# Attention scores from high and low parts of q and k in three fp32r products, and one chunk of a projection moved ahead of them

## The chip, the cores and the metric

The kernel runs on one core of a Trainium2 chip. The metric is the time of one execution on the device in microseconds (us), the median of several runs. The engines are TensorE (PE in the rows; PEld are its weight loads), VectorE (DVE), ScalarE (ACT), GpSimd (POOL) and SyncE (SP, which issues DMAs). Each works through its own list of instructions in order and waits on semaphores for the others.

## The reference

One layer of a hybrid decoder, for 528 prompt positions (16 learned meta tokens and 512 tokens) and 8 decoded tokens, 536 columns in all, d_model 1024, in float32:

```
x = x + 1/2 * SwiGLU_1(RMSNorm(x))
z = RMSNorm(x) @ w_in          -> u (pool group, 512) | q (8 heads of 64) | k | v (2 heads of 64)
q, k: RMSNorm over the head, rotation of the first quarter of the head
pool group: causal trailing means over 2/4/8/16 positions minus the token, a linear map per group, a scale
attention: sliding window of 128 in blocks of 128 queries x 256 keys, sinks:
  s = einsum('bnqhgd,bnkhd->bnhgqk', qb, k_band) * SCALE        (q, k in float32)
  p = exp(s - m) / (sum(exp(s - m)) + exp(sink - m));   o = p @ v
x = x + concat(pool, attention) @ w_out
x = x + 1/2 * SwiGLU_2(RMSNorm(x))
```

## The kernel before

Activations lie transposed: 128 channels on the partitions, positions along the free dimension. Wherever a product is large, both operands are kept as a high part (the value rounded to fp32r) and a low part (value minus high part), and three fp32r matmuls, hi x hi, lo x hi and hi x lo, are added up in PSUM (`product`, L612). ACT makes the high parts by a copy to fp32r, DVE the low parts by a subtraction (`split_hi`, `split_lo`).

The change is in the mixing stage between the two half FFNs, some 100 of the 877 us. Ten projections of w_in run in the order k, v, q0 to q3, u0 to u3 (`project(m, ks)`, m from 0 to 9), each of eight chunks of 128 rows of w_in; `ks` says which chunks, so that a projection can be cut and other work of TensorE put between. q0 to q3 each hold two heads, one on partitions 0 to 63 and one on 64 to 127, and so does k.

For x from 1 to 4 (q0 to q3; x = 0 is k) the way from a projection to the scores is: DVE evacuates it into `gate` (`take_z(x)`), ACT writes the gained values `zg` and the squares `zsq` (`spread_z(x)`), SP sends four DMAs that put the rotation's partner rows into `partner` (`send_partner(x)`), GpSimd multiplies `zg` by the cosines into `hid`, DVE multiplies `partner` by the sines into `sq` (`rotate(x)`, L1862), and GpSimd adds the two (L2123) into `qT`. For x = 0 the sum stays in `hid`, and DVE multiplies it by the inverse norm into `kT` (L1868). `zg`, `zsq` and `partner` have two buffers each, `hid` and `sq` one. The norm of q goes into the scores as a factor (`qscale`).

There are eight steps of attention, i = 0 to 7: block t = i % 4 of 128 queries, and two heads of each group, q0 and q1 for i < 4, q2 and q3 after. Of each step TensorE does `scores(i)` (four products of 64 rows, 128 x 256, L960, in plain fp32), `turn_probs(i)` (eight transposes, L969) and `attend(i)` (L978). DVE does `maxima(i)` (L1913 to L1919) and `normalise(i)` (L1925 to L1930, writes `prob`), ACT `exps(i)` (L1393), `out_probT(i)` (L1401, PSUM to `probT`) and `out_hi(i)`, DVE `out_lo(i)`. `attend(i)` waits for `probT`, `turn_probs(i)` for `prob`.

Each engine's order is written out by hand. TensorE around the first steps:

```
project(4, [5, 6, 7]); project(5, half[0]); scores(0); scores(1)
project(5, half[1]); project(6, half[0])
turn_probs(0); scores(2); project(6, [4]); attend(0); project(6, [5]); ...
turn_probs(1); scores(3); attend(1); ...
```

Steps 3, 4 and 6 run `turn_probs`, `scores` of the next step, `attend` without a break; steps 5 and 7 have `pool_map` (L933) between `turn_probs` and `scores`. (Steps are named here by their scores.) DVE runs `rotate(2)`, the reciprocal of the first norms, `take_z(3)`, `split_next(4)`, `maxima(0)`, `rotate(3)`, `maxima(1)`, `normalise(0)`, `take_z(4)`, `normalise(1)`. ACT runs `spread_z(2)`, `q_root(0)`, `split_next(4)`, `spread_z(3)`, `exps(0)`, `exps(1)`, `spread_z(4)`, `out_probT(0)`. After q3's add GpSimd copies the decoded tokens' queries into `dq` (L2129) and goes on to the pool group's window sums (L2106).

Of the kernel before, what the change touches and what calls it, by code (L numbers as in the profile page):

```python
# [39 lines left out]
P = 128  # L40
# [108 lines left out]
def build(nc, a):  # L149
# [52 lines left out]
    assert prob_end <= t4_end  # L202
    sq, _ = place("sq", [P, NT])
    sqsum, _ = place("sqsum", [P, NT])
    fixed, _ = place("fixed", [P, N_FIXED])
# [31 lines left out]
    qT, o = place("qT", [P, GQ, NOUT], offset=xlo_end)  # L237
# [26 lines left out]
    dscore, o = place("dscore", [HD, P], offset=o)  # L264
    assert o <= raw_at
# [71 lines left out]
    dq_ready = sem("dq_ready")  # L337
    dscores_filled = sem("dscores_filled")
# [261 lines left out]
    def _(pe):  # L600
# [320 lines left out]
        project(5, half[0])  # L921
# [15 lines left out]
        def scores(i):  # L937

            t = i % QT
            if i == 0:  # L940
                pe.wait_ge(rot_ready, 3)
                pe.wait_ge(root_ready, 4)
            elif i == 2:
                pe.wait_ge(evacuated, E_USE["q3"] + 1)
            elif i > 2:
                pe.wait_ge(olo_ready, i - 2)
            if i == 3:
                pe.wait_ge(root_ready, 5)
            elif i == 4:
                pe.wait_ge(rot_ready, 5)  # L950
# [6 lines left out]
            for k in (0, 2, 1, 3):  # L957
                g, j = head_of(i, k)
                rows = slice(g * HD, (g + 1) * HD)
                last = nc.tensor.matmul(dst[k], qT[rows, j, t * P:(t + 1) * P], kT[rows, t * P:(t + 2) * P],  # L960
                                        start=True, stop=True)
                if j % 2:
                    last.then_inc(scored, 1)
# [20 lines left out]
        def decode_scores(part):  # L984

            if part == 0:
                pe.wait_ge(newk_placed, 1)
                pe.wait_ge(dq_ready, KVH)
# [52 lines left out]
        project(5, half[1])  # L1041
# [69 lines left out]
    def _(act):  # L1111
# [275 lines left out]

        def exps(i):
# [31 lines left out]
        spread_z(2)  # L1420

# [5 lines left out]

        q_root(0).then_inc(root_ready, 1)
        act.wait_ge(warmed, 2)
        nc.scalar.activation(warm[:, :], eps[:, :], ACT.Exp).then_inc(warmed, 1)  # L1430
        split_next(4)
        spread_z(3)
        exps(0)
        exps(1)
        spread_z(4)
# [9 lines left out]
        out_probT(1)  # L1445
        split_next(6)
# [66 lines left out]
    def _(dve):  # L1513
# [357 lines left out]

        def pool_mean(g):
# [91 lines left out]
        nc.vector.tensor_copy(ckT[:, :, WIN - 1], kT[:, PAD + TP:PAD + NT]).then_inc(newk_placed, 1)  # L1964
        rotate(2)
        dve.wait_ge(root_ready, 4)
        half_q = QT * KVH * 2
        nc.vector.reciprocal(qnrm[:, 1, 0:half_q], qnrm[:, 0, 0:half_q]).then_inc(inv_ready, 1)
        take_z(3)
        split_next(4)  # L1970
# [19 lines left out]
        maxima(3)  # L1990
        dve.wait_ge(dscores_filled, 1)
# [97 lines left out]
    def _(pool):  # L2089
# [23 lines left out]
        for x in range(5):  # L2113
            cols = slice(0 if x == 0 else META, NT)
            pool.wait_ge(zg_ready, x + 1)
            if x == 1:
                pool.wait_ge(qk_ready, 1)
            nc.gpsimd.tensor_tensor(hid[:, cols], zg[:, x % 2, cols], cosT[:, cols], ALU.mult
# [3 lines left out]
            dst = hid[:, :] if x == 0 else qT[:, x - 1, :]  # L2122
# [113 lines left out]
```

## Time and profile before

| | us |
|---|---|
| median of 3 runs (879.41 to 879.66) | 879.43 |
| the profiled execution's own time | 879.43 |
| its span, from the first to the last instruction | 877.5 |
| TensorE busy | 872.0 (99%) |
| DVE busy | 659.4 (75%) |
| ACT busy | 394.0 (45%) |
| GpSimd busy | 32.4 (4%) |

The span is the profile's; the time of an execution has 1.9 us more around it. Times in rows are counted from the span's start. The ends of matmuls are modelled, and neighbours overlap in the rows, so what an operation of TensorE costs is read from start to start. A row of the timeline gives in brackets how long the engine was idle before it, and who released it.

### The profile page before, as it was taken

Reading aid. Unit: us, or ns where it says so; the run is one execution under the profiler, and the core shown is the slowest. Engines: PE = TensorE matmul, PEld = TensorE weight load, DVE = VectorE, ACT = ScalarE, POOL = GpSimd, SP = SyncE. Lnnn points to the kernel's source line nnn. Section 1 sums busy time; section 2 is a strip of 40 time slices with the busy share of each in tenths; the row PEclk is TensorE's granted clock in tenths of the full one; section 3 lists DMA queues with packets and bytes.
Section 4 is the critical chain, followed back from the end, with each engine's and each line's share of the span. In section 5 each row is a group of like instructions: output and inputs, shape, how many; then the busy total and the mean of one; then the engine's idle time right before and its main releaser. Section 6 shows DMA issues by size and latency. Waiting matters only on the chain.

```text
span 877.5 us, 17072 instructions
## 1 busy us (share of the span) xinstructions
PE 872.0 (99%) x7088; PEld 857.4 (98%) x7088; DVE 659.4 (75%) x979; ACT 394.0 (45%) x639; POOL 32.4 (4%) x37
## 2 busy tenths in 40 slices
PE   9999999999999999999999999999999999999998
PEld 8999999999999999999888999999999999999998
DVE  7979547997569986754887697996479975799754
ACT  8635313554224553443754465554125542255420
POOL 0000000000000000012423000000000000000000
PEclk9999999999999999999999999999999999999999
DMA  7333313332424322522321405324233324333241
GB/s 261 107 121 117 136 60 121 121 121 85 145 68 162 121 77 84 190 76 59 106 73 62 155 27 169 120 82 172 73 121 120 121 85 145 115 122 124 85 122 61
DMA packets 43180, 98.57 MB, mean 112 GB/s; under 512 B 4288, under 2 KB 5056, under 8 KB 43104
## 3 DMA queue, kind: packets, MB, share of 16 engines
q1 hardware_dynamic: 41376, 95.01, 32.7%
q10 hardware_dynamic: 1728, 2.48, 0.8%
q8 instruction: 56, 0.92, 0.4%
q14 instruction: 20, 0.16, 0.1%
HBM read 93.53 MB, written 3.60 MB: 111 GB/s over the span
## 4 chain that ended last, share of the span: by engine, by line
PE 97%; DVE 1%; DMA 1%; issue 0%; ACT 0%; SPq 0%; DVEq 0%
PE ps L612 45%; PE ps L740 15%; PE ps L742 15%; PE ps L741 15%; PE ps L642 1%; PE ps L978 1%; PE ps L960 1%; PE ps L969 1%; PE ps L799 1%; DMA raw<-gu 1%; PE ps L933 0%; PE ps L883 0%; PE ps L657 0%; DVE wlo L1533 0%; DVE hlo L1660 0%; DVE hid L1653 0%
## 5 line engine op out<-in xcount | busy, mean ns | idle before, releaser
L740 PE MATMUL ps<-xhi,whi 128*128 128x260 f32 (+1 forms) x1092 | 310.2, 284 | 0.1
L742 PE MATMUL ps<-xhi,wlo 128*128 128x260 f32 (+1 forms) x1092 | 310.0, 284 | 0.0
L741 PE MATMUL ps<-xlo,whi 128*128 128x260 f32 (+1 forms) x1092 | 309.5, 283 | 0.0
L740 PEld LDWEIGHTS ps<-xhi,whi 128*128 128x128 f32 x1092 | 205.3, 188 | 0.8 <-issue 0.6
L742 PEld LDWEIGHTS ps<-xhi,wlo 128*128 128x128 f32 x1092 | 205.4, 188 | 0.0
L741 PEld LDWEIGHTS ps<-xlo,whi 128*128 128x128 f32 x1092 | 205.4, 188 | 0.0
L1604 DVE TENSOR_TENSOR wlo<-full,whi 128x1024 fp32r<-128x1024 f32 (+1 forms) x117 | 160.4, 1395 | 0.0
L1129 ACT CAST whi<-raw 128x1024 fp32r<-128x1024 f32 (+1 forms) x75 | 75.2, 1003 | 154.9 <-PE ps L612 148.0
L612 PE MATMUL ps<-hhi,whi 128*128 128x268 f32 (+1 forms) x690 | 140.4, 285 | 0.3
L612 PE MATMUL ps<-hlo,whi 128*128 128x268 f32 (+1 forms) x690 | 140.1, 284 | 0.0
L612 PE MATMUL ps<-hhi,wlo 128*128 128x268 f32 (+1 forms) x690 | 139.7, 284 | 0.0
L612 PEld LDWEIGHTS ps<-hhi,whi 128*128 128x128 f32 x690 | 106.8, 188 | 1.1 <-DVE hlo L1660 1.1
L612 PEld LDWEIGHTS ps<-hhi,wlo 128*128 128x128 f32 x690 | 107.0, 188 | 0.0
L612 PEld LDWEIGHTS ps<-hlo,whi 128*128 128x128 f32 x690 | 106.8, 188 | 0.0
L1533 DVE TENSOR_TENSOR wlo<-raw,whi 128x1024 fp32r<-128x1024 f32 (+1 forms) x75 | 90.3, 1205 | 16.8 <-ACT whi L1129 16.5
L1700 DVE SCALAR_TENSOR_TENSOR gate<-ps,rstd 128x536 f32<-128x536 f32 (+1 forms) x47 | 33.3, 708 | 81.7 <-PE ps L612 81.2
L1189 ACT CAST whi<-full 128x1024 fp32r<-128x1024 f32 x39 | 41.0, 1052 | 106.3 <-issue 89.5
L612 PE MATMUL ps<-xhi,whi 128*128 128x268 f32 (+1 forms) x288 | 60.9, 293 | 0.0
L612 PE MATMUL ps<-xhi,wlo 128*128 128x268 f32 (+1 forms) x288 | 58.7, 285 | 0.0
L612 PE MATMUL ps<-xlo,whi 128*128 128x268 f32 (+1 forms) x288 | 58.5, 285 | 0.0
L1203 ACT CAST whi<-full 128x1536 fp32r<-128x1536 f32 x39 | 57.8, 1483 | 0.0
L1589 DVE TENSOR_TENSOR full<-full 128x1024 f32<-128x1024 f32 x39 | 47.4, 1217 | 0.0
(194 smaller groups left out, 1071.1 us busy)
## 6 DMA issues: line engine op xcount, KB each, us to landing
full<-gu SPq DMA_DIRECT2D x78, 512.0 KB, 4.3
raw<-d SPq DMA_DIRECT2D x32, 448.0 KB, 3.3
full<-gu SPq DMA_DIRECT2D x39, 256.0 KB, 2.7
raw<-d SPq DMA_DIRECT2D x16, 512.0 KB, 3.4
raw<-w_in SPq DMA_DIRECT2D x10, 512.0 KB, 3.7
raw<-gu SPq DMA_DIRECT2D x9, 512.0 KB, 3.7
raw<-w_out SPq DMA_DIRECT2D x8, 512.0 KB, 3.9
xT<-x SPq DMA_DIRECT2D x8, 268.0 KB, 5.5
```

What stands on the lines that cost most here:

```text
L612: last = nc.tensor.matmul(dst[:, h, 0:n], w[:, kk, :], x(k, lo, h), start=(k == begin and i == 0), stop=(k == end and i == 2))
L642: done = nc.tensor.matmul(dst[:, h, 0:n], w[:, c % 2, t, :], x(k, lo, h), start=(first and t == 0 and i == 0), stop=(last and t == KD - 1 ...
L740: nc.tensor.matmul(dst, whi_t, xhi_t, start=(first and pr == 0), stop=False, skip_group_check=True)
L741: nc.tensor.matmul(dst, whi_t, xlo_t, start=False, stop=False, skip_group_check=True)
L742: last = nc.tensor.matmul(dst, wlo_t, xhi_t, start=False, stop=(pr == KC - 1), skip_group_check=True)
L1129: nc.scalar.copy(whi_of(c)[:, 0:t, :], raw[:, c % RAW, 0:t, :]).then_inc(whi_ready, 1)
L1189: nc.scalar.copy(whi7[:, i % 2, 0:2, :], full[:, i % 3, 0:2, :]).then_inc(hi_ready[0], 1)
L1203: nc.scalar.copy(whi7[:, i % 2, 4:7, :], full[:, i % 3, 4:7, :]).then_inc(hi_ready[2], 1)
L1533: nc.vector.tensor_tensor(wlo_of(c)[:, 0:t, :], raw[:, c % RAW, 0:t, :], whi_of(c)[:, 0:t, :].bitcast(F32), ALU.subtract).then_inc(wlo_rea ...
L1589: nc.vector.tensor_tensor(full[:, r, 1:5:3, :], full[:, r, 1:5:3, :], full[:, r, 0:7:6, :], ALU.add).then_inc(added, 1)
L1604: nc.vector.tensor_tensor(wlo7[:, i % 3, b, :], full[:, i % 3, b, :], whi7[:, i % 2, b, :].bitcast(F32), ALU.subtract).then_inc(lo_ready[g ...
L1700: nc.vector.scalar_tensor_tensor(out=halves(gate[:, cols], n), in0=pair[d % 2][:, :, 0:n], scalar=-0.5, in1=halves(rstd[:, cols], n), op0= ...
```

## The change

The scores are computed from high and low parts: `khi`, `klo` for all of k, `qhi[:, j]` and `qlo[j]` for the 520 columns of each q. Each of the four fp32 products of a step becomes three fp32r matmuls of the same shape (hi x hi, lo x hi, hi x lo), interleaved by pairs of heads so that neighbours lie on different halves of the rows. GpSimd's add now leaves every q in `hid`; ACT copies it into `qhi` (`q_hi(x)`), and DVE (x = 1, 2, 4) or GpSimd (x = 3) subtracts to get `qlo` (`q_lo(x)`). Since `hid` is one buffer, GpSimd's multiply for the next q waits for the low part of the one before. ACT copies `kT` into `khi`, DVE subtracts to get `klo`. `dq` is filled after each q by two small copies, instead of two larger ones at the end. On TensorE, five chunks of `project(5)` now lie ahead of the first scores instead of four, and three behind them. The new tiles lie over buffers that are free in this stage.

```diff
@@ -918,7 +930,7 @@
         project(4, [2, 3, 4])
         q_sums(1)
         project(4, [5, 6, 7])
-        project(5, half[0])
+        project(5, [0, 1, 2, 3, 4])
 
         def use(name):
 
@@ -938,7 +950,9 @@
 
             t = i % QT
             if i == 0:
-                pe.wait_ge(rot_ready, 3)
+                pe.wait_ge(klo_ready, 1)
+                pe.wait_ge(qlo_ready[0], 1)
+                pe.wait_ge(qlo_ready[1], 1)
                 pe.wait_ge(root_ready, 4)
             elif i == 2:
                 pe.wait_ge(evacuated, E_USE["q3"] + 1)
@@ -947,20 +961,25 @@
             if i == 3:
                 pe.wait_ge(root_ready, 5)
             elif i == 4:
-                pe.wait_ge(rot_ready, 5)
+                pe.wait_ge(qlo_ready[2], 1)
+                pe.wait_ge(qlo_ready[3], 1)
                 pe.wait_ge(dscores_kept, 2)
             elif i == 6:
                 pe.wait_ge(dprobs_kept, 1)
             elif i == 7:
                 pe.wait_ge(douts_kept, 1)
             dst = [banks_of[i % 3][:, j // 2, (j % 2) * 2 * P:(j % 2 + 1) * 2 * P] for j in range(GQ)]
-            for k in (0, 2, 1, 3):
-                g, j = head_of(i, k)
-                rows = slice(g * HD, (g + 1) * HD)
-                last = nc.tensor.matmul(dst[k], qT[rows, j, t * P:(t + 1) * P], kT[rows, t * P:(t + 2) * P],
-                                        start=True, stop=True)
-                if j % 2:
-                    last.then_inc(scored, 1)
+            queries, keys = slice(t * P, (t + 1) * P), slice(t * P, (t + 2) * P)
+            for pair_of_heads in ((0, 2), (1, 3)):
+                for part in range(3):
+                    for k in pair_of_heads:
+                        g, j = head_of(i, k)
+                        rows = slice(g * HD, (g + 1) * HD)
+                        q = qlo[j][rows, queries] if part == 1 else qhi[rows, j, queries]
+                        last = nc.tensor.matmul(dst[k], q, (klo if part == 2 else khi)[rows, keys],
+                                                start=(part == 0), stop=(part == 2))
+                        if part == 2 and j % 2:
+                            last.then_inc(scored, 1)
 
         def turn_probs(i):
             pe.wait_ge(prob_ready, i + 1)
@@ -985,7 +1004,7 @@
 
             if part == 0:
                 pe.wait_ge(newk_placed, 1)
-                pe.wait_ge(dq_ready, KVH)
+                pe.wait_ge(dq_ready, KVH * GQ)
                 pe.wait_ge(probT_ready, 2)
             for b in range(part * NDEC // 2, (part + 1) * NDEC // 2):
                 last = nc.tensor.matmul(turn[:, 1, b * HEADS:(b + 1) * HEADS], ckT[:, b, :], dq[:, b, :, :],
@@ -1038,7 +1057,7 @@
 
         scores(0)
         scores(1)
-        project(5, half[1])
+        project(5, [5, 6, 7])
         project(6, half[0])
 
         turn_probs(0)
@@ -1385,6 +1404,11 @@
                 sq_x = nc.scalar.activation(dzsq[:, :, x - 1], gate[:, TP:NT], ACT.Square)
             sq_x.then_inc(zg_ready, 1)
 
+        def q_hi(x):
+
+            act.wait_ge(rot_ready, x + 1)
+            nc.scalar.copy(qhi[:, x - 1, :], hid[:, META:NT]).then_inc(qhi_ready, 1)
+
         def exps(i):
             act.wait_ge(nmax_ready, i + 1)
             s = i % 2
@@ -1418,6 +1442,9 @@
         spread_z(1)
         split_next(3)
         spread_z(2)
+        act.wait_ge(pads_zero, 1)
+        act.wait_ge(qk_ready, 1)
+        nc.scalar.copy(khi[:, :], kT[:, :]).then_inc(khi_ready, 1)
 
         def q_root(r):
 
@@ -1425,13 +1452,16 @@
             act.wait_ge(nsum_filled, 4 + r)
             return nc.scalar.activation(qnrm[:, 0, cols], nsum[:, r, cols], ACT.Sqrt, scale=1.0, bias=eps64[:, 0:1])
 
+        q_hi(1)
         q_root(0).then_inc(root_ready, 1)
         act.wait_ge(warmed, 2)
         nc.scalar.activation(warm[:, :], eps[:, :], ACT.Exp).then_inc(warmed, 1)
         split_next(4)
+        q_hi(2)
         spread_z(3)
         exps(0)
         exps(1)
+        q_hi(3)
         spread_z(4)
 
         out_probT(0)
@@ -1443,6 +1473,7 @@
                              ).then_inc(root_ready, 1)
 
         out_probT(1)
+        q_hi(4)
         split_next(6)
         out_hi(1)
         exps(3)
@@ -1869,6 +1900,12 @@
                                                    nsum[:, h, 0:right - left], ALU.mult)
                 last.then_inc(qk_ready, 1)
 
+        def q_lo(x):
+
+            dve.wait_ge(qhi_ready, x)
+            nc.vector.tensor_tensor(qlo[x - 1][:, :], hid[:, META:NT], qhi[:, x - 1, :].bitcast(F32), ALU.subtract
+                                    ).then_inc(qlo_ready[x - 1], 1)
+
         def pool_mean(g):
 
             p, w = g, WINDOWS[GROUPS[g]]
@@ -1962,11 +1999,15 @@
         split_next(3)
         rotate(1)
         nc.vector.tensor_copy(ckT[:, :, WIN - 1], kT[:, PAD + TP:PAD + NT]).then_inc(newk_placed, 1)
+        q_lo(1)
         rotate(2)
+        dve.wait_ge(khi_ready, 1)
+        nc.vector.tensor_tensor(klo[:, :], kT[:, :], khi[:, :].bitcast(F32), ALU.subtract).then_inc(klo_ready, 1)
         dve.wait_ge(root_ready, 4)
         half_q = QT * KVH * 2
         nc.vector.reciprocal(qnrm[:, 1, 0:half_q], qnrm[:, 0, 0:half_q]).then_inc(inv_ready, 1)
         take_z(3)
+        q_lo(2)
         split_next(4)
         dve.wait_ge(inv_ready, 4)
         maxima(0)
@@ -1988,6 +2029,7 @@
         nc.vector.reciprocal(qnrm[:, 1, half_q:2 * half_q], qnrm[:, 0, half_q:2 * half_q])
         nc.vector.reciprocal(dnrm[:, 1:2], dnrm[:, 0:1]).then_inc(inv_ready, 1)
         maxima(3)
+        q_lo(4)
         dve.wait_ge(dscores_filled, 1)
         for g in range(KVH):
             last = nc.vector.tensor_copy(
@@ -2115,20 +2157,26 @@
             pool.wait_ge(zg_ready, x + 1)
             if x == 1:
                 pool.wait_ge(qk_ready, 1)
+            elif x:
+                pool.wait_ge(qlo_ready[x - 2], 1)
             nc.gpsimd.tensor_tensor(hid[:, cols], zg[:, x % 2, cols], cosT[:, cols], ALU.mult
                                     ).then_inc(cos_ready, 1)
             pool.wait_ge(cos_ready, x + 1)
             pool.wait_ge(sin_ready, x + 1)
-            dst = hid[:, :] if x == 0 else qT[:, x - 1, :]
-            nc.gpsimd.tensor_tensor(dst, hid[:, cols], sq[:, cols], ALU.add).then_inc(rot_ready, 1)
+            nc.gpsimd.tensor_tensor(hid[:, cols], hid[:, cols], sq[:, cols], ALU.add).then_inc(rot_ready, 1)
 
             pool.wait_ge(rot_ready, x + 1)
-        pool.wait_ge(pads_zero, 6)
-        for g in range(KVH):
-            rows = slice(g * HD, (g + 1) * HD)
-            nc.gpsimd.tensor_copy(dq[rows, :, g, :], qT[rows, :, SEQ:NOUT].rearrange("p j b -> p b j")
-                                  ).then_inc(dq_ready, 1)
-            pool.wait_ge(dq_ready, g + 1)
+            if x == 1:
+                pool.wait_ge(pads_zero, 6)
+            for g in range(KVH) if x else ():
+                rows = slice(g * HD, (g + 1) * HD)
+                nc.gpsimd.tensor_copy(dq[rows, :, g, x - 1], hid[rows, TP:NT]).then_inc(dq_ready, 1)
+            if x:
+                pool.wait_ge(dq_ready, KVH * x)
+            if x == 3:
+                pool.wait_ge(qhi_ready, x)
+                nc.gpsimd.tensor_tensor(qlo[x - 1][:, :], hid[:, META:NT], qhi[:, x - 1, :].bitcast(F32), ALU.subtract
+                                        ).then_inc(qlo_ready[x - 1], 1)
 
         def pool_lo(g):
 
```

The remaining lines of the diff place the new tiles and make the semaphores `khi_ready`, `klo_ready`, `qhi_ready` and `qlo_ready[0..3]`.

## Rows read from the trace of the kernel before

**Rows 1.** The page: the chain that ended last, by engine, share of the span.

```profile
PE 97%; DVE 1%; DMA 1%; issue 0%; ACT 0%; SPq 0%; DVEq 0%
```

**Rows 2.** Engines by stage: window, length, busy us PE PEld DVE ACT POOL, clock, DMA.

```profile
413.00:475.00 62.00, 61.81 (x478) 51.47 (x476) 50.28 (x156) 37.55 (x105) 20.29 (x19) 1.00 0.21 65
```

**Rows 3.** Waits, 400 to 480: waiting line, released by: total, times, longest us.

```profile
PEld ps L978 <- ACT probT L1401: 1.7, 4, 0.4
...
PEld ps L969 <- DVE prob L1930: 0.2, 1, 0.2
```

**Rows 4.** TensorE's timeline around one step: start, duration, line, records.

```profile
445.15 1.14 PE L933 MATMUL ps<-gate,poolw 128*128 128x260 f32 x4
446.23 1.13 PE L960 MATMUL ps<-kT,qT 64*128 64x256 f32 x8
447.29 1.08 PE L978 MATMUL ps<-probT,tok 128*64 128x256 f32 x8
...
451.08 0.41 PE L612 MATMUL ps<-xlo,whi 128*128 128x268 f32 x2
451.33 0.41 PE L612 MATMUL ps<-xhi,wlo 128*128 128x268 f32 x2
```

**Rows 5.** TensorE's timeline, first steps of attention.

```profile
413.37 2.00 PE L960 MATMUL ps<-kT,qT 64*128 64x256 f32 x16
...
421.43 1.09 PE L969 MATMUL ps<-fixed,prob 128*128 128x128 f32 x8
...
424.45 1.08 PE L978 MATMUL ps<-probT,tok 128*64 128x256 f32 x8
...
430.80 1.13 PE L960 MATMUL ps<-kT,qT 64*128 64x256 f32 x8
431.97 1.08 PE L978 MATMUL ps<-probT,tok 128*64 128x256 f32 x8
```

**Rows 6.** ACT's timeline, 411 to 449.

```profile
411.60 0.73 ACT L1381 ACTIVATE zg<-gate,fixed 128x520 f32<-128x520 f32 x1
...
412.75 0.20 ACT L1385 ACTIVATE dzsq<-gate 128x8 f32<-128x8 f32 x1
...
422.02 0.73 ACT L1381 ACTIVATE zg<-gate,fixed 128x520 f32<-128x520 f32 x1
...
423.28 0.99 ACT L1401 COPY probT<-ps 128x1024 f32<-128x1024 f32 x1
...
430.90 1.01 ACT L1401 COPY probT<-ps 128x1024 f32<-128x1024 f32 x1 [1.26 <-PE ps L969]
...
448.72 0.63 ACT L1411 CAST mhi<-act_gate 128x520 fp32r<-128x520 f32 x1
```

**Rows 7.** GpSimd's timeline, 406 to 450.

```profile
406.14 1.30 POOL L2123 TENSOR_TENSOR qT<-hid,sq 128x520 f32<-128x520 f32 x1 [5.75 <-DVE sq L1862]
...
410.34 1.32 POOL L2123 TENSOR_TENSOR qT<-hid,sq 128x520 f32<-128x520 f32 x1 [1.53 <-DVE sq L1862]
...
428.34 2.17 POOL L2123 TENSOR_TENSOR qT<-hid,sq 128x520 f32<-128x520 f32 x1 [3.51 <-DVE sq L1862]
...
449.49 1.30 POOL L2136 TENSOR_TENSOR mlo<-act_gate,mhi 128x520 fp32r<-128x520 f32 x1 [0.91 <-ACT mhi L1411]
```

**Rows 8.** DVE's timeline, 409 to 452.

```profile
409.50 0.70 DVE L1862 TENSOR_TENSOR sq<-partner,sinT 128x520 f32<-128x520 f32 x1 [3.41 <-DMA partner<-zg]
...
417.06 0.70 DVE L1862 TENSOR_TENSOR sq<-partner,sinT 128x520 f32<-128x520 f32 x1 [0.23 <-DMA partner<-zg]
...
420.15 1.22 DVE L1930 TENSOR_TENSOR prob<-ps,small 128x1024 f32<-128x1024 f32 x1
...
428.11 1.22 DVE L1533 TENSOR_TENSOR wlo<-raw,whi 128x1024 fp32r<-128x1024 f32 x1
...
435.72 0.29 DVE L1993 COPY dscoreT<-ps 128x32 f32<-128x32 f32 x2 [0.98 <-PE ps L991]
...
449.98 1.90 DVE L1533 TENSOR_TENSOR wlo<-raw,whi 128x1024 fp32r<-128x1024 f32 x1
```

More of the change, by code:

```diff
@@ L201, in build @@
     prob, prob_end = place("prob", [P, 2, GQ, 2 * P], offset=upn_at)
-    assert prob_end <= t4_end
+    qlo0, o = place("qlo0", [P, NOUT], F32R, offset=prob_end)
+    assert o <= t4_end
     sq, _ = place("sq", [P, NT])
+    sqsum_at = at[0]
     sqsum, _ = place("sqsum", [P, NT])
+    qlo1, _ = place("qlo1", [P, NOUT], F32R, offset=sqsum_at)
     fixed, _ = place("fixed", [P, N_FIXED])
@@ L236, in build @@
     assert o <= xlo_at
-    qT, o = place("qT", [P, GQ, NOUT], offset=xlo_end)
+    qlo2, _ = place("qlo2", [P, NOUT], F32R, offset=xhi_end + NT * 4)
+    qhi, o = place("qhi", [P, GQ, NOUT], F32R, offset=xlo_end)
+    qlo3, _ = place("qlo3", [P, NOUT], F32R, offset=o)
+    qlo = [qlo0, qlo1, qlo2, qlo3]
     cosT, o = place("cosT", [P, NT], offset=o)
@@ L264, in build @@
     dscore, o = place("dscore", [HD, P], offset=o)
+    khi, o = place("khi", [P, PAD + NT], F32R, offset=o)
+    klo, o = place("klo", [P, PAD + NT], F32R, offset=o)
     assert o <= raw_at
@@ L337, in build @@
     dq_ready = sem("dq_ready")
+    khi_ready = sem("khi_ready")
+    klo_ready = sem("klo_ready")
+    qhi_ready = sem("qhi_ready")
+    qlo_ready = [sem(f"qlo_ready{x}") for x in range(1, 5)]
     dscores_filled = sem("dscores_filled")
```

## The prediction

> **What bounds the kernel now.** I read the chain of waits first, then the table of engines by stage, then the list of waits around the scores, and then the timelines of TensorE, ACT, GpSimd and DVE, one after the other. The chain gives 97% of the span to TensorE [rows 1], so the time changes by what TensorE computes and by what makes it wait. In the 62 us from the first scores to the last `attend` it is busy 61.81, at a granted clock of 1.00; DVE is busy 50.28 of these, ACT 37.55, GpSimd 20.29 [rows 2]. The reader should see that TensorE has next to no idle time here. The list of waits says how near it comes to having some: the weight loads of `attend` (L978) waited four times for ACT's copy `probT`, and those of `turn_probs` (L969) once for DVE's `prob` [rows 3]. At these five places work taken from TensorE buys nothing, and lateness of the other engines costs its full length.
>
> **The products.** In one step TensorE does four fp32 products of 64 rows by 256 columns, and the next operation starts 1.06 after the first [rows 4]. They leave eight records, and these take 1.13, as long as the four records of `pool_map` just before them, which use all 128 rows and 260 columns (1.14): so two products on the two halves of the rows run at once. `pool_map`'s two fp32 products last 1.08 from start to start, while two fp32r matmuls of 268 columns start 0.25 before the next two, 0.12 each: one fp32 product costs a little over four fp32r matmuls. Two pairs of products in four passes each are eight slots of 256 columns, 0.96 of the 1.06; two pairs in three are six. That saves 0.24 at most, and as the first slot and the change to and from half rows may cost more around short matmuls, I take 0.2. From below the saving is negative: no row shows fp32r on half of the rows, and if the twelve went one by one they would take 12 x 0.12 = 1.44 for 0.96 now. I keep the pairs, because the same halves run together in fp32.
>
> The Trainium skill, FP8 and Floating Point Precision, section TensorE Precision Notes, says that true FP32 takes four passes through the array, high and low parts against each other. By it a step of three products would cost three quarters of 1.06, a saving of 0.27; the rows above give a little less.
>
> **What a faster step is worth.** The scores stand between `turn_probs` and `attend`. In step 3 the scores start at 430.80 and `attend` at 431.97 [rows 5], 0.11 later than their 1.06 would allow; `probT` starts at 430.90 and lasts 1.01 [rows 6], to 0.06 before `attend`. There ACT's copy sets the start, not the scores. Steps 3, 4 and 6 have this form (the four waits of [rows 3] hold them), and gain nothing. Steps 5 and 7 have `pool_map` between, which covers the copy: these gain 0.2 each, 0.4 together. Steps 0, 1 and 2 lie before the new waits, and gain only if these don't bind.
>
> **The moved chunk.** A chunk of `project(5)` is six matmuls of 0.12: the first scores come 0.72 later, at 414.09 instead of 413.37 [rows 5]. The work is the same, but 7 chunks, not 8, now cover the way from the first scores to `turn_probs(0)`.
>
> **The new chain ahead of the first scores.** One step after the other, with durations of the nearest rows:
> - GpSimd's add for q_1 ends at 407.44 as before [rows 7]. `q_hi(1)` is a cast of 520 columns, 0.63 as L1411 [rows 6]: to 408.10. `q_lo(1)` is a DVE operation on two 520 column inputs in SBUF, 0.70 as L1862 [rows 8]: to 408.84.
> - `hid` is one buffer, so GpSimd's multiply for q_2 waits for `q_lo(1)`: with 0.14 for the signal (L1862 ends at 410.20, GpSimd's add starts at 410.34) and 1.30, from 408.98 to 410.28.
> - DVE's own multiply for q_2 gets its partner rows at 409.50, in the middle of that. The rows show what happens then: GpSimd's add at 428.34 took 2.17, ending 1.18 after DVE's L1533 that had begun first (428.11, 1.22); L1533 at 449.98 took 1.90, ending 1.09 after GpSimd's subtraction (449.49, 1.30) [rows 7, 8]. The second waits for the whole of the first, then needs its own time less 0.13. So DVE's multiply ends at 410.28 + 0.57 = 410.85.
> - `klo` follows at once on DVE: 648 columns, between 0.70 for 520 and 1.22 for 1024, so 0.83, to 411.60. GpSimd's add for q_2, woken at 410.99, is now second: 411.60 + 1.18 = 412.78 instead of 411.66.
> - `q_hi(2)` then runs 412.81 to 413.44, `q_lo(2)` to 414.18. The first scores may start at 414.24; TensorE is there at 414.09. This wait is 0.15.
> - The larger loss is behind `q_hi(2)` in ACT's queue. `spread_z(3)` started at 411.60 [rows 6] and now starts some 0.53 after the cast did, at 413.34: 1.74 later. Its `zg` goes through four DMAs; their rows reached DVE at 417.06, where DVE had waited 0.23 for them [rows 8], 4.11 after `zg_ready` (412.75 + 0.20). Now that is 418.80. `rotate(3)` stands in DVE's queue between `maxima(0)` and `maxima(1)`, so all behind it is 1.74 late: `prob` ends at 423.11, not 421.37, and `turn_probs(0)` starts at 423.17, not 421.43. TensorE would be there at about 420.8 (421.43 less its wait of 0.2 and two faster steps), so it idles over 2 us.
> - ACT's `q_hi(3)` is new between `exps(1)` and `spread_z(4)`. `exps(1)`, which ended shortly before 422.02, ends 1.74 late; I let the cast start at 423.55, and `spread_z(4)` 0.53 later, at 424.08 instead of 422.02. `probT(0)` moves from 423.28 to 425.34 and ends at 426.33; `attend(0)` starts at 426.39 instead of 424.45: 1.94 late.
>
> The Trainium skill, SBUF — State Buffer, section Who interferes with whom, says that a DVE instruction with two SBUF inputs and a GpSimd instruction that reads SBUF hold one port in turn, each for its whole length. The trace agrees with 2.17 for 1.30 and 1.90 for 1.22; by the rule each of the new subtractions is such an instruction.
>
> **What is hidden.** `khi` (ACT, about 0.75) runs while ACT waits for the sums of q. The `dq` copies, now eight small ones, lie where GpSimd waits for other engines, as does its `qlo3`. `q_hi(4)` lies before `split_next(6)`, far ahead of its use. `q_lo(4)` has DVE's idle 0.98 before the copy of the decode scores [rows 8] as cover; but GpSimd's four window adds run then, and if one holds the port the copy is up to 0.6 late and TensorE up to 0.4. I take 0.1.
>
> **Sum.** 1.94 - 0.4 + 0.1 = +1.6 us. The profiled execution took 879.43, which is the median of the runs; its span is 877.5 and the 1.9 around it does not change. Forecast: 881.1.
>
> **Rivals.**
> - *No collision at the port.* Without it q_2's add ends at 411.65, `q_hi(2)` runs when ACT is free at 411.68, `spread_z(3)` is 0.61 late, `attend(0)` 0.81, and the sum is 0.81 - 0.4 = +0.4: 879.9. For it: rows show the effect only with operations of 1024 columns on DVE. Against: the two orders of start both show it.
> - *The pairs don't overlap in fp32r* (the other side: slower). Each step is 1.44 - 0.96 = 0.48 longer. Steps 3, 4 and 6 outgrow ACT's copy by 0.48 - 0.11, 1.1 together, 5 and 7 lose 0.48 each, and step 2 makes `attend(0)` 0.2 later: 1.94 + 0.1 + 1.1 + 1.0 + 0.2 = +4.3: 883.8. It decides from the point where a step takes longer than now, 1.06 + 0.11 in steps 3, 4 and 6. For it: no row with this form. Against: eight records in the time of four.
> - *The saving shows and the chain is in time.* Eight steps at 0.2 less, no new wait: -1.6, 877.8; even then it barely differs from no change. Against it: DVE's `prob` was already the last to come [rows 3], and the move puts the scores 0.72 later.
> - *The change saves nothing on TensorE* (fp32r at 256 columns as slow as fp32) would be 12 us more; the fp32r rows at 260 and 268 columns speak against it, and I leave it in the tail.
>
> **How the numbers follow.** 0.2%, 1.76 us, is about what a measurement of this kernel tells from no change. The forecast (0.60) lies just inside it; its own range is 880.3 to 881.9, and two fifths of it are beyond 881.2. No collision 0.17; no overlap 0.13; saving shown 0.07; the rest 0.03 is slower. Slower by over 0.2%: 0.6 x 0.4 + 0.13 + 0.03 = 0.40. Faster: the part of the third rival that goes beyond its sum, 0.05. Between: 0.55. A range from 879.0 to 883.4 leaves out the second and the third rival, 0.2.
>
> **What would show it.** Right: `turn_probs(0)` near 423.2 waiting for `prob`, `maxima(1)` late behind a `rotate(3)` that waits for the partner DMA near 418.8, `spread_z(3)` behind `q_hi(2)`, GpSimd's add for q_2 lengthened next to `klo`; steps of scores near 0.86 with records two at a time; `attend` in steps 3, 4 and 6 still 0.06 after `probT`. Wrong: scores records one at a time; an add for q_2 that ends by 411.7; or TensorE without a wait ahead of `turn_probs(0)`.

## The result, and the profile after

| | before | after |
|---|---|---|
| median of 22 runs each (us) | 879.54 (878.93 to 881.54) | 881.57 (881.06 to 883.02) |
| ratio, with its 95% interval | 1 | 1.0022 (1.0016 to 1.0027) |
| profiled execution: time, span (us) | 879.43, 877.5 | 881.67, 879.9 |
| TensorE, DVE, ACT, GpSimd busy (us) | 872.0, 659.4, 394.0, 32.4 | 870.9, 663.4, 396.8, 35.7 |

The change costs 2.0 us, 0.22%: the forecast was 881.1 within 879.0 to 883.4. The interval of the ratio reaches to both sides of the 0.2% at which the prediction drew its line between no change and slower.

In some executions of nearly every kernel here, the one before too, TensorE's mean granted clock is 0.994 to 0.998 and the time 0.6 to 4.2 us longer; where tenths count, medians are therefore also given over the executions at 1.000 alone (879.4 to 879.5 for the kernel before in the four groups of runs below, 881.48 for the changed one).

A q with an underscore counts by x: q_1 is q0, q_2 is q1, and so on.

The page of the changed kernel, the busy line and the chain that ended last:

```profile
PE 870.9 (99%) x7120; PEld 857.7 (97%) x7120; DVE 663.4 (75%) x983; ACT 396.8 (45%) x644; POOL 35.7 (4%) x44
...
PE 93%; DVE 3%; DMA 1%; ACT 1%; issue 1%; SPq 1%; POOL 0%; DVEq 0%; ACTq 0%; POOLq 0%
```

TensorE has 1.1 us less to do, and its share of the chain fell from 97% to 93% [rows 1]: the chain now runs through DVE, ACT and a DMA for a while. The stage from the first scores to the last `attend`, with the columns of [rows 2]:

```profile
414.00:477.00 63.00, 59.81 (x502) 51.17 (x502) 52.88 (x158) 38.99 (x110) 22.25 (x22) 1.00 0.21 64
```

Where TensorE was idle for 0.19 us of 62.00, it is now idle for 3.19 of 63.00, at the same clock of 1.00. DVE has 2.6 us more in this stage, ACT 1.4, GpSimd 2.0. The waits of 400 to 480 (waiting line, released by: total, times, longest) say where the idle time lies:

```profile
DVE sq L1893 <- DMA partner<-zg: 2.9, 3, 1.2
...
PE ps L988 <- DVE prob L1967: 1.7, 1, 1.7
...
POOL hid L2162 <- DVE qlo L1906: 1.1, 1, 1.1
...
PE ps L997 <- ACT probT L1425: 0.8, 4, 0.3
...
PE ps L979 <- DVE qlo L1906: 0.3, 1, 0.3
...
PE ps L1017 <- DVE dscoreT L2035: 0.2, 1, 0.2
```

The largest is `turn_probs(0)` (L988, L969 before), 1.7 us behind DVE's `prob`. Ahead of that, DVE waited longer for the partner rows of x = 3 (1.06 in the timeline below, 0.23 in [rows 8]); its three waits for partner rows together are shorter than before, 2.9 against 4.7, since `q_lo(1)` takes up part of the one for q_2. GpSimd has a wait it did not have, its multiply behind a low part. The timeline of all engines along that way, and around `decode_turn` (L1017). This trace runs 0.27 us behind the other before the change begins (the sums of q_1's squares start at 404.27 before, at 404.54 here), so 0.27 is to be taken from its times before they are set beside [rows 5 to 8]:

```profile
406.41 1.30 POOL L2166 TENSOR_TENSOR hid<-hid,sq 128x520 f32<-128x520 f32 x1 [5.75 <-DVE sq L1893]
...
407.75 0.62 ACT L1410 CAST qhi<-hid 128x520 fp32r<-128x520 f32 x1 [1.47 <-POOL hid L2166]
...
408.40 0.70 DVE L1906 TENSOR_TENSOR qlo<-hid,qhi 128x520 fp32r<-128x520 f32 x1 [2.05 <-ACT qhi L1410]
...
409.28 1.30 POOL L2162 TENSOR_TENSOR hid<-zg,cosT 128x520 f32<-128x520 f32 x1 [1.05 <-DVE qlo L1906]
...
409.77 1.36 DVE L1893 TENSOR_TENSOR sq<-partner,sinT 128x520 f32<-128x520 f32 x1 [0.67 <-DMA partner<-zg]
...
411.06 0.82 DVE L2005 TENSOR_TENSOR klo<-kT,khi 128x648 fp32r<-128x648 f32 x1
...
411.28 1.77 POOL L2166 TENSOR_TENSOR hid<-hid,sq 128x520 f32<-128x520 f32 x1 [0.70 <-DVE sq L1893]
...
413.08 0.63 ACT L1410 CAST qhi<-hid 128x520 fp32r<-128x520 f32 x1 [1.12 <-POOL hid L2166]
...
413.62 0.73 ACT L1400 ACTIVATE zg<-gate,fixed 128x520 f32<-128x520 f32 x1
...
414.73 0.39 PE L979 MATMUL ps<-khi,qhi 64*128 64x256 f32 x2 [0.30 <-DVE qlo L1906]
414.93 0.31 PE L979 MATMUL ps<-khi,qlo 64*128 64x256 f32 x2
...
416.35 0.51 PE L624 MATMUL ps<-xhi,whi 128*128 128x260 f32 x2
...
419.08 0.70 DVE L1893 TENSOR_TENSOR sq<-partner,sinT 128x520 f32<-128x520 f32 x1 [1.06 <-DMA partner<-zg]
...
422.16 1.23 DVE L1967 TENSOR_TENSOR prob<-ps,small 128x1024 f32<-128x1024 f32 x1
...
423.44 1.09 PE L988 MATMUL ps<-fixed,prob 128*128 128x128 f32 x8 [1.69 <-DVE prob L1967]
...
424.46 0.39 PE L979 MATMUL ps<-khi,qhi 64*128 64x256 f32 x2
...
425.37 0.51 PE L624 MATMUL ps<-xhi,whi 128*128 128x268 f32 x2
...
425.56 1.02 ACT L1425 COPY probT<-ps 128x1024 f32<-128x1024 f32 x1
...
426.63 1.08 PE L997 MATMUL ps<-probT,tok 128*64 128x256 f32 x8 [0.25 <-ACT probT L1425]
...
434.51 3.59 POOL L2148 TENSOR_TENSOR wsum<-wsum 128x528 f32<-128x528 f32 x3
...
436.85 1.80 DVE L1906 TENSOR_TENSOR qlo<-hid,qhi 128x520 fp32r<-128x520 f32 x1
...
438.58 0.28 DVE L2035 COPY dscoreT<-ps 128x32 f32<-128x32 f32 x2
...
438.91 0.30 PE L1017 MATMUL ps<-fixed,dscoreT 128*64 128x128 f32 x1 [0.22 <-DVE dscoreT L2035]
```

Read it from the top. `q_hi(1)`, `q_lo(1)` and GpSimd's multiply for q_2 follow each other at once; DVE's `sq` for q_2 takes 1.36 instead of 0.70, beside that multiply; GpSimd's add takes 1.77 instead of 1.32, beside `klo`; `q_hi(2)` comes behind it, and `spread_z(3)` (`zg`) behind that, 1.75 later than before (413.62 less 0.27, against 411.60 in [rows 6]). From there it is the old way with everything late: partner rows, `prob`, `turn_probs(0)`, `probT`, `attend(0)`, the last one 1.91 later than in [rows 5]. The scores themselves are shorter: records come two at a time, the two steps from 414.73 to 416.35 take 1.62 where they took 1.93 (413.37 to the next operation at 415.30 before).

Set against the trace of before, start by start with the 0.27 taken off, TensorE is late by 1.73 at `turn_probs(0)`, 1.90 at `attend(0)` and `attend(1)`, 2.28 at `decode_turn`, 2.44 at the scores of step 5, 2.29 behind them, and 2.16 at the end.

### The profile page after: what moved, and what is told of

It reads as the page before. It is cut to its first block, busy times and chain, and to the rows that moved or that the text cites. A ratio compares the mean times of both kernels' runs of the same rounds, so it can differ in the third digit from the quotient of the medians.

```text
span 879.9 us, 17156 instructions
## 1 busy us (share of the span) xinstructions
PE 870.9 (99%) x7120; PEld 857.7 (97%) x7120; DVE 663.4 (75%) x983; ACT 396.8 (45%) x644; POOL 35.7 (4%) x44
## 4 chain that ended last, share of the span: by engine, by line
PE 93%; DVE 3%; DMA 1%; ACT 1%; issue 1%; SPq 1%; POOL 0%; DVEq 0%; ACTq 0%; POOLq 0%
PE ps L624 42%; PE ps L752 15%; PE ps L754 15%; PE ps L753 15%; PE ps L654 1%; PE ps L997 1%; DMA xT<-x 1%; PE ps L811 1%; DVE ps L1950 0%; PE ps L945 0%; DMA partner<-zg 0%; SPq L566 0%; PE ps L988 0%; DVE wlo L1564 0%; PE ps L669 0%
```

## The experiments

Theory A is the prediction's: the time is lateness in the queues of ACT, DVE and GpSimd, given by the chain ahead of `spread_z(3)` and `q_hi(3)` and by the port that DVE and GpSimd hold in turn; the products gain a little in the steps that no wait covers. Its rivals: the moved chunk costs the time, or the products cost it, or the single `hid` buffer and the port have no part in it. "At clock 1.000" below is the median over those executions, with their number; the figure in brackets is the same for the kernel before, run on the same chip. Offsets of a trace are starts against the trace of before, with the difference at the sums of q_1's squares taken off.

**Only the moved chunk** (`e1_chunk_only`).

```diff
-        project(5, half[0])
+        project(5, [0, 1, 2, 3, 4])
...
-        project(5, half[1])
+        project(5, [5, 6, 7])
```

> The kernel before with only one part of the change: five chunks of the projection of q3 ahead of the first scores, three behind; the scores stay in plain fp32. Theory A (the new chain through hid, the casts and the partner DMA makes prob late): the chunk by itself moves the first scores 0.72 later, uses up the 0.23 that rotate(3) waited for its partner rows, and makes turn_probs(0) 0.5 later; the kernel takes 0.4 to 0.5 us more than before, about 880.0. Theory B (the moved chunk is the loss): nearly all of the 2 us, about 881.4.

880.10, ratio 1.0002 (0.9993 to 1.0011); at clock 1.000 also 880.10 (879.41). In its trace the first scores are 0.72 late and `turn_probs(0)` 0.41, with a wait of 0.44 for `prob`; the end is 0.47 late. So the chunk has a price by itself, 0.5 us in the trace and 0.7 between the medians at clock 1.000, a fifth to a third of what the whole change costs.

**The change without the moved chunk** (`e2_four_ahead`), the same lines put back in the changed kernel.

> The changed kernel with the chunk moved back: four chunks ahead of the first scores, as before. Theory A: the first scores still can't start before qlo of q2, so TensorE waits some 0.9 instead of 0.3 ahead of them; maxima(1) is set by the partner DMA, so turn_probs(0) comes at the same time, and the kernel takes as long as the changed one, within 0.2 us. Theory B: most of the loss is gone, 1.5 us less than the changed kernel.

881.50, ratio 1.0018 (1.0009 to 1.0026); at clock 1.000 881.28 (879.41). Its trace is late by 1.75 at `turn_probs(0)`, 1.91 at `attend(0)` and 2.19 at the end, as the changed kernel's is: within the change the chunk is free, since the new chain is later than it.

**The new chain with fp32 scores** (`e3_fp32_scores`): four fp32 products of the high parts, the low parts still made but not used.

```diff
-                for part in range(3):
...
+                last = nc.tensor.matmul(dst[k], qhi[rows, j, queries].bitcast(F32), khi[rows, keys].bitcast(F32),
+                                        start=True, stop=True)
```

> The changed kernel with its whole chain of casts and subtractions, but the scores as single plain fp32 products of the high parts; the low parts are made and left out of the scores. Theory A: the three fp32r products save 0.16 per step, but only where nothing else sets the start of what follows, in steps 5 and 7: this run takes 0.3 to 0.4 us more than the changed kernel. Rival C (the three products themselves, with twelve weight loads for four, are the loss): this run is faster than the changed kernel by 1 us or more.

881.83, ratio 1.0025 (1.0016 to 1.0033); at clock 1.000 also 881.83, 0.35 above the changed kernel. `turn_probs(0)` and `attend(0)` are late by 1.75 and 1.91 as there. The lateness belongs to the preparation of the operands; the three products themselves give some 0.35 back (single executions lie between 881.43 and 882.79, so its second digit is open).

**`rotate(3)` and `q_hi(3)` later** (`e4_late_rotate`): in DVE's order `rotate(3)` from between `maxima(0)` and `maxima(1)` to behind `take_z(4)`, in ACT's `q_hi(3)` from ahead of `spread_z(4)` to ahead of `exps(2)`.

```diff
         maxima(0)
-        rotate(3)
         maxima(1)
         normalise(0)
         take_z(4)
+        rotate(3)
```

> The changed kernel with two steps in another order: DVE does rotate(3) behind take_z(4) instead of between maxima(0) and maxima(1), and ACT does q_hi(3) ahead of exps(2) instead of ahead of spread_z(4). No work is added or taken away. Theory A: maxima(1) no longer waits for the partner DMA and probT(0) no longer for q_hi(3); turn_probs(0) comes about 2 us earlier than in the changed kernel, attend(0) too; the kernel is 1.8 to 2.3 us faster than the changed one, at or a little below the kernel before (879.2 to 879.6). Rival C (more work on DVE, ACT and GpSimd in general, or the products): no gain.

881.12, ratio 1.0015 (1.0007 to 1.0024); at clock 1.000 881.00. Half of this came true: `turn_probs(0)` is 0.06 late and `attend(0)` 0.07 early, so it is through these two orders that the whole 1.9 reaches TensorE. But the expected end was missed by 1.4 us (881.00, where 879.6 was the most expected). Timeline of DVE and TensorE further on:

```profile
428.37 2.30 DVE L1564 TENSOR_TENSOR wlo<-raw,whi 128x1024 fp32r<-128x1024 f32 x1
...
435.91 1.81 DVE L1906 TENSOR_TENSOR qlo<-hid,qhi 128x520 fp32r<-128x520 f32 x1
...
437.97 0.42 PE L1017 MATMUL ps<-fixed,dscoreT 128*64 128x128 f32 x1 [1.51 <-DVE dscoreT L2035]
```

With `q_hi(3)` later, GpSimd's multiply and add for q_4 moved into DVE's `split_next(5)` (2.30 instead of 1.22), `q_lo(4)` again lay beside window adds (1.81), and `decode_turn` waited 1.51. From 0.07 early at `attend(1)` TensorE went to 1.61 late at `decode_turn`: the gain was given back 16 us later. (In this execution the clock fell during that wait, so what lies behind it is not compared.)

**The products alone** (`e5_products_alone`): the kernel before with `qT` in fp32r, `khi` copied from `kT`, and one tile of zeros for every low part of q and one for that of k, all made by ACT or by GpSimd's existing add.

```diff
+                for part in range(3):
+                    for k in pair_of_heads:
...
+                        q = qlo0[rows, queries] if part == 1 else qT[rows, j, queries]
```

> The kernel before with its own chain and order (GpSimd's adds write fp32r queries, no q_hi, no q_lo on DVE or GpSimd, four chunks ahead), but with three fp32r products for each fp32 one; the low parts are zeros, so the products with low parts add nothing (left out: what the low parts hold). Theory A (a step of scores is 0.155 us shorter, and only steps without a bound copy keep it): end 0.3 to 0.6 us earlier in the trace, the ratio within 0.1% of 1, near 879.1. Rival B (the products themselves cost the 2 us, by a slower mode on half rows or a change of mode): 1.5 to 2 us slower, 881 to 881.5. Rival C (all eight steps keep their gain): 1.2 us faster or more, 878.3.

879.21, ratio 0.9992 (0.9983 to 1.0001); at clock 1.000 879.24 (879.52). In the trace the end is 0.38 early. TensorE's timeline at steps 3 and 5:

```profile
430.49 0.38 PE L969 MATMUL ps<-khi,qT 64*128 64x256 f32 x2
...
431.67 1.08 PE L987 MATMUL ps<-probT,tok 128*64 128x256 f32 x8 [0.20 <-ACT probT L1410]
...
445.93 0.39 PE L969 MATMUL ps<-khi,qT 64*128 64x256 f32 x2
...
446.84 1.08 PE L987 MATMUL ps<-probT,tok 128*64 128x256 f32 x8
```

In step 5 the next operation starts 0.91 after the scores, where it took 1.06 [rows 4]. In step 3 it starts 1.18 after, 0.20 of it a wait for `probT`; it took 1.17 before [rows 5]. The gains by step, from the offsets: 0.13 at step 2, 0.14 at step 5, 0.15 at step 7; steps 0 and 1 end in a wait of 0.34 ahead of `turn_probs(0)`, and steps 3, 4 and 6 in waits of 0.20, 0.19 and 0.19 for `probT`. This is the ceiling of the change as the kernel is ordered: 0.3 us between the medians at clock 1.000, 0.4 in the trace. The interval of the ratio alone does not tell it from nothing.

**`klo` not on DVE** (`e6_no_klo`): zeros from ACT.

```diff
+        nc.scalar.activation(klo[:, :], khi[:, :].bitcast(F32), ACT.Copy, scale=0.0).then_inc(klo_ready, 1)
...
-        nc.vector.tensor_tensor(klo[:, :], kT[:, :], khi[:, :].bitcast(F32), ALU.subtract).then_inc(klo_ready, 1)
```

> The changed kernel, with klo filled with zeros by ScalarE instead of by VectorE's subtraction (left out: high q times low k). Theory A (VectorE's subtraction holds the port against GpSimd's add for q_2): the add takes 1.30 instead of 1.77, q_hi(2), spread_z(3), turn_probs(0) and the end come 0.45 us earlier than in the changed kernel, 881.1. Rival B (the add is long for another reason, or the chain runs elsewhere): the add keeps its 1.77, nothing moves, 881.5.

881.07, ratio 1.0013 (1.0004 to 1.0022); at clock 1.000 881.05. GpSimd's add for q_2 and `turn_probs(0)` in its timeline:

```profile
411.18 1.31 POOL L2166 TENSOR_TENSOR hid<-hid,sq 128x520 f32<-128x520 f32 x1 [0.70 <-DVE sq L1895]
...
422.89 1.10 PE L988 MATMUL ps<-fixed,prob 128*128 128x128 f32 x8 [1.60 <-DVE prob L1969]
```

The add takes 1.31 with no `klo` beside it, and `turn_probs(0)`, `attend(0)` and the end are 1.27, 1.44 and 1.76 late instead of 1.73, 1.90 and 2.16. So 0.46 of the 1.9 is the meeting of `klo` and the add.

**A second `hid`** (`e7_two_hid`): q_1 and q_3 are summed in another free tile.

```diff
+    def hid_of(x):
+        return act_gate if x % 2 else hid
...
-            elif x:
-                pool.wait_ge(qlo_ready[x - 2], 1)
+            elif x > 2:
+                pool.wait_ge(qlo_ready[x - 3], 1)
```

> The changed kernel with a second buffer for hid, so that GpSimd's multiply for q_2 no longer waits for q_lo(1). Theory A (the chain from q_lo(1) through GpSimd to q_hi(2) and spread_z(3) sets turn_probs(0)): the multiply starts some 1.4 us earlier, VectorE's multiply for q_2 takes 0.70 again, the add meets klo still, and turn_probs(0) and the end come 0.5 to 0.6 us earlier than in the changed kernel, 880.9 to 881.1. Rival B (the single buffer is not on the path: q_hi(2) alone in front of spread_z(3) costs it): less than 0.1 us, 881.5.

881.21, ratio 1.0010 (1.0000 to 1.0019); at clock 1.000 881.18. `attend(0)` is 1.54 late, the end 1.80: a gain of 0.36, against 0.5 to 0.6 expected. GpSimd and DVE in its timeline:

```profile
408.44 1.30 POOL L2165 TENSOR_TENSOR hid<-zg,cosT 128x520 f32<-128x520 f32 x1
408.54 1.76 DVE L1909 TENSOR_TENSOR qlo<-act_gate,qhi 128x520 fp32r<-128x520 f32 x1 [2.04 <-ACT qhi L1413]
...
411.05 1.77 POOL L2169 TENSOR_TENSOR hid<-hid,sq 128x520 f32<-128x520 f32 x1 [1.31 <-DVE sq L1896]
```

The multiply no longer waits for `q_lo(1)`; instead `q_lo(1)` waits for the multiply (1.76 instead of 0.70), and the add still meets `klo`.

**`q_lo(4)` not on DVE** (`e8_no_qlo4`): zeros from ACT behind `q_hi(4)`.

```diff
+        nc.scalar.activation(qlo[3][:, :], khi[:, 0:NOUT].bitcast(F32), ACT.Copy, scale=0.0).then_inc(qlo_ready[3], 1)
...
-        q_lo(4)
```

> The changed kernel with q3's low part filled with zeros by ScalarE behind q_hi(4), instead of by VectorE's q_lo(4) ahead of the copy of the decode scores (left out: low q3 times high k). Theory A (q_lo(4), held by GpSimd's window adds, makes the copy and decode_turn late by 0.4 us, and this is not regained): turn_probs(0) and attend(0) stay, decode_turn has no wait for VectorE, the end comes 0.4 us earlier, 881.1. Rival B (a lateness there is taken up by a later wait): the end does not move, 881.5.

881.26, ratio 1.0016 (1.0007 to 1.0025); at clock 1.000 881.05 (5 executions), 0.43 below the changed kernel, as theory A expects. Its trace shows no loss from `attend(1)` to `decode_turn` (3.13 and 3.12 late), where the changed kernel lost 0.38; but this isn't a clean comparison, since TensorE's clock fell in the profiled execution behind the wait ahead of `turn_probs(0)`, and a later TensorE leaves DVE's copy more time. By windows, columns as in [rows 2]:

```profile
422.00:424.00 2.00, 0.50 (x5) 0.50 (x6) 1.95 (x3) 2.00 (x10) 0.00 (x0) 1.00 0.00 0
424.00:426.00 2.00, 2.00 (x19) 1.61 (x18) 1.78 (x5) 2.00 (x5) 1.31 (x1) 0.78 0.00 0
426.00:428.00 2.00, 2.00 (x10) 1.57 (x11) 1.88 (x10) 1.58 (x2) 1.30 (x1) 0.50 0.09 17
```

**Everything rearranged** (`e9_combo`, complete again): the edits of e4 and e7, with `q_hi(3)` behind `split_next(5)`, GpSimd's low part of x = 3 behind its last add, and:

```diff
+        q_hi(4)
         out_probT(1)
-        q_hi(4)
...
+        q_lo(4)
         take_u(0)
...
-        q_lo(4)
```

(in its expectation, "the low part of q3's neighbour q_3" is that of x = 3.)

> The changed kernel, complete, with its new work put elsewhere: rotate(3) behind take_z(4) on VectorE, q_hi(3) behind ScalarE's split_next(5), q_hi(4) into ScalarE's idle time ahead of out_probT(1), q_lo(4) into VectorE's idle time ahead of take_u(0), a second buffer for hid, and GpSimd's low part of q3's neighbour q_3 behind its last add. Theory A (the 2 us are lateness in the queues, not work of TensorE): turn_probs(0) within 0.2 us of the kernel before, no wait for VectorE ahead of decode_turn, end 0.2 to 0.5 us earlier than before, 879.0 to 879.3. Rival B (VectorE and GpSimd have no room for the new work in this stage, wherever it is put): a wait of about 1 us appears elsewhere, 880.3 to 881.

882.31, ratio 1.0025 (1.0015 to 1.0034); at clock 1.000 881.34 (4 executions). `turn_probs(0)` and `attend(0)` come 0.25 and 0.37 early. GpSimd, DVE and TensorE after that:

```profile
430.54 1.29 POOL L2180 TENSOR_TENSOR qlo<-act_gate,qhi 128x520 fp32r<-128x520 f32 x1
...
430.71 1.68 DVE L1909 TENSOR_TENSOR qlo<-hid,qhi 128x520 fp32r<-128x520 f32 x1 [1.92 <-ACT qhi L1413]
...
438.10 0.30 PE L1020 MATMUL ps<-fixed,dscoreT 128*64 128x128 f32 x1 [1.96 <-DVE dscoreT L2038]
```

My placing was wrong: DVE waited 1.92 for `q_hi(4)`, then for GpSimd's low part, all ahead of `take_u(0)` which had been ready; what lies behind it on DVE, the copy of the decode scores last, came 2 us late. On the way an operation of 128 x 4 (L1959), which takes 0.16 in the kernel before, took 1.21 beside the last window add. It is rival B's mechanism at twice its size.

**The same with three moved chunks, and the chunks alone** (`e10_combo_moves`, `e11_before_moves`): in steps 3, 4 and 6 one chunk goes between the scores and `attend`.

```diff
         scores(4)
+        project(7, [4])
         attend(2)
-        project(7, half[1])
+        project(7, [5, 6, 7])
```

> The same, and in steps 3, 4 and 6 one chunk of the next projection moves from behind attend to between the scores and attend. Theory A (there ScalarE's copy probT sets the start of attend, so a chunk in front of it covers the copy and the shorter scores show): attend in steps 3, 4 and 6 no longer waits, 0.15 to 0.2 us each, 0.5 us less than the kernel without the moves, 878.5 to 878.8. Rival B (the later attend delays ScalarE's and VectorE's next work by as much): no gain, or a new wait ahead of a turn_probs.

> The kernel before with those three moved chunks alone, as a control. Theory A (each of its three attends waits about 0.1 us for the copy): 0.1 to 0.3 us less than the kernel before, 879.2 to 879.4. Rival B (the moves themselves are worth the whole 0.5 us, and the fp32r products nothing): as fast as the kernel with both.

882.20 and 880.16, ratios 1.0036 (1.0023 to 1.0049) and 1.0008 (0.9999 to 1.0016); at clock 1.000 881.21 (3 executions) and 880.04 (879.47). In the first the chunk of step 3 waits 1.97 for the same late `take_u(0)`, so it can't tell whether the moves are worth anything. The control lost 0.6 where a gain was expected. In its profiled execution the clock fell ahead of step 3, so what it lost there stays open; behind that its trace shows 0.36, of which 0.09 in step 4, 0.18 at `pool_map(0)` and 0.09 in step 6.

**Rearranged once more** (`e12_combo2`): e9 with `take_u(0)` first again, `q_hi(4)` behind `out_probT(1)`, and GpSimd making the low parts of x = 3 and x = 4.

```diff
+            if x == 4:
+                pool.wait_ge(qhi_ready, 3)
+                nc.gpsimd.tensor_tensor(qlo[2][:, :], hid_of(3)[:, META:NT], qhi[:, 2, :].bitcast(F32), ALU.subtract
+                                        ).then_inc(qlo_ready[2], 1)
             pool.wait_ge(cos_ready, x + 1)
...
+        pool.wait_ge(qhi_ready, 4)
+        nc.gpsimd.tensor_tensor(qlo[3][:, :], hid_of(4)[:, META:NT], qhi[:, 3, :].bitcast(F32), ALU.subtract
+                                ).then_inc(qlo_ready[3], 1)
```

> The rearranged kernel once more, without the moved chunks: take_u(0) on VectorE is again ahead of everything that waits for q_hi(4); q_hi(4) stands behind out_probT(1); GpSimd makes the low parts of both of the last two queries, one between its multiply and its add for q_4, where it was idle for 2.4 us, the other ahead of its window adds. Theory A (VectorE's q_lo(4), which waited 1.9 us in front of take_u(0), cost the 2 us ahead of decode_turn): turn_probs(0) and attend(0) 0.25 and 0.35 us earlier than in the kernel before, decode_turn between 0.3 us earlier and 0.3 us later, end 0.1 to 0.6 us earlier, 878.9 to 879.4. Rival B (the later window adds hold VectorE's small operations and the copy of the decode scores comes late again): a wait of over 0.5 us ahead of decode_turn or turn_probs(3), 879.8 or more.

879.94, ratio 1.0003 (0.9994 to 1.0012); at clock 1.000 879.93 (879.54). The same sums in 1.6 us less than the changed kernel, but not under the kernel before: 0.4 above it at clock 1.000. `turn_probs(0)`, `attend(0)` and `decode_turn` are early by 0.25, 0.38 and 0.19; then 0.9 goes in one wait (timeline of GpSimd, DVE and TensorE):

```profile
434.56 4.56 POOL L2150 TENSOR_TENSOR wsum<-wsum 128x528 f32<-128x528 f32 x3
...
437.88 1.26 DVE L2050 SCALAR_TENSOR_TENSOR dsmall<-dsmall,nsink 64x1 f32<-64x1 f32 x1
...
445.80 1.14 PE L948 MATMUL ps<-gate,poolw 128*128 128x260 f32 x4 [0.89 <-DVE up L1880]
```

A DVE operation of one column, 0.15 in the kernel before, stood 1.26 beside the last window add, which the new low part had pushed back; DVE has no slack between there and `take_u(1)` (`up`), on which `pool_map(0)` waits. That is rival B, one operation further on than it was expected.

## Why the prediction was right, and by how much it was off

**The products.** Right in kind: records two at a time, no gain where `probT` sets `attend` (e5: waits of 0.20, 0.19, 0.19 in steps 3, 4 and 6), a gain in steps 5 and 7. The term was mis-sized: 0.2 taken for a step, 0.15 measured, so 0.3 for the two instead of 0.4. The slots are 0.12 as assumed, six of them 0.71; but a step takes 0.91 in all (424.46 to 425.37), 0.20 more, at its two ends, where the step in fp32 took 1.06. The estimate from the Trainium skill, FP8 and Floating Point Precision, section TensorE Precision Notes (four passes for true FP32), was 0.27 in the prediction; the measured 0.15 is less than that. The rivals without overlap and without a saving are out, and the one that put the gain of all eight steps at 1.6 is too: with no new chain at all (e5) it is 0.4. (The 12 us of the rival without a saving follow from no row: three products for one at the price of fp32 would be 2.12 more in a step, 17 in eight.)

**The moved chunk.** Its 0.72 came to the hundredth at the first scores in e1. Alone it costs 0.5 to 0.7 (e1), in the change nothing (e2).

**The chain.** All its times, taken off by 0.27, lie within 0.05 of the forecast but one: GpSimd's add for q_2 ends at 412.78 (412.78 forecast), `zg` starts at 413.35 (413.34), partner rows at 418.81 (418.80), `turn_probs(0)` at 423.17 (423.17), `probT` at 425.29 (425.34), `attend(0)` at 426.36 (426.39). The one is the first scores, 414.46 against 414.24: `q_lo(2)` ended at 414.18 as forecast, but TensorE started 0.28 after it, where 0.06 had been taken. It had no effect, since TensorE waits at `turn_probs(0)` anyway; the wait there was 1.69, not the over 2 that was forecast, as part of it had been spent ahead of the scores.

**The port.** The rival without a collision is out. The add beside `klo` took 1.77 and without it 1.31, and the end moved by 0.40 (e6); with the buffer doubled, which gained 0.36, the other collision only changed sides (e7). What would be left of the 1.9 without any collision, 0.8 by the prediction's rival, was not tested: no run takes away both, or `q_hi(2)` alone. That the second of two such operations waits is what the Trainium skill, SBUF — State Buffer, section Who interferes with whom, says of operations with two SBUF inputs beside GpSimd's, and the trace agrees down to one column (1.26 for 0.15 in e12).

**`q_lo(4)`.** The term that was furthest off. 0.1 was taken between 0 and 0.4, and it was the upper bound: GpSimd's adds ran until 438.10 (434.51 + 3.59), `q_lo(4)` could start its own part only then and ended at 438.65, and `decode_turn` went from 1.90 late to 2.28. e8 without it is 0.43 faster. The trace before had a row that spoke for such a wait. GpSimd's four adds stand side by side in it, 78 ns apart, and a small DVE operation met one of them:

```profile
432.31 3.59 POOL L2106 TENSOR_TENSOR wsum<-wsum 128x528 f32<-128x528 f32 x3
...
434.23 0.31 DVE L1916 SCALAR_TENSOR_TENSOR small<-small,nsink 128x4 f32<-128x4 f32 x1
434.58 0.16 DVE L1919 TENSOR_TENSOR small<-small,fixed 128x4 f32<-128x4 f32 x1
```

The first took 0.31 instead of 0.16, to the end of the second add of the three; the next got through between two adds. So how long `q_lo(4)` would wait hung on where it fell; it fell 0.05 behind the start of the last add, and waited for nearly the whole of it.

**The sum.** 1.90 + 0.38 for `decode_turn` + 0.19 in small waits behind it (0.13 of it `pool_map(0)`, for DVE) - 0.15 - 0.16 gives the 2.16 of the end, against 1.94 + 0.1 - 0.4 forecast. The span grew by 2.4, of which 0.27 had gone before the change began.

Hidden as forecast were `khi`, the `dq` copies, GpSimd's low part and `q_hi(4)`. What stays open is whether some order of these queues gets below the kernel before: the best complete one here (e12) can't be told from it by its interval and lies 0.4 above it at clock 1.000, and the ceiling of e5 is 0.3 to 0.4 us.

## What to carry to other kernels

Where one engine has 99% of the span, a change that takes a little from it and gives the others new work is priced by the queues of the others: write their chain out instruction by instruction, with the port as one of the queues, and ask of each new operation what stands behind it. A wait that is removed at the head of a stage comes back further on if the new work is only pushed behind other work (e4, e9); find the slack that it goes into first. Where work lies among back-to-back GpSimd operations, price every DVE operation there that has two inputs in SBUF at up to the whole of one of them, however small it is.

## What was not expected of the hardware

A DVE operation of one column waits like a wide one for the rest of the GpSimd operation that it meets: 64 x 1 took 1.26 instead of 0.15 (e12), and 128 x 4 took 0.59 and 0.63 (e4) and 1.21 (e9) instead of 0.16.

TensorE's granted clock falls from 1.00 (2.4 GHz) to 0.50 (1.2 GHz) for a few us in a part of the executions: 30 of 108 of the kernel before show a mean of 0.998, 4 of 22 of the changed one, 5 of 11 of e4, and 7 and 8 of 11 of e9 and e10 one of 0.998 or less. In the traces of e3, e4 and e9 TensorE falls 1.3 to 1.5 us behind over it. An idle TensorE ahead of it doesn't decide it: in e8 it fell right behind an idle time of 1.7 us, the changed kernel's profiled execution kept 1.00 through the same one, and in the control e11 it fell with TensorE busy without a gap:

```profile
428.00:430.00 2.00, 2.00 (x20) 1.97 (x18) 1.42 (x2) 1.70 (x3) 1.57 (x1) 0.89 0.51 199
430.00:432.00 2.00, 2.00 (x10) 1.68 (x9) 1.45 (x4) 0.00 (x0) 1.71 (x4) 0.50 0.71 137
```

What sets it off was not tried.
